# A two-layer diffusion backbone on one core: scaling ahead of the output split, squares in quarter buffers, and token transposes ahead of the logits

## The chip, the core and the metric

The kernel runs on one core of a Trainium2 chip. The metric is the device time of one launch in microseconds (us). Three runs of the kernel before took 1660.24, 1662.55 and 1663.87 us, median 1662.55.

## What is computed

Two layers of a transformer trunk over 256 latent tokens and 256 context tokens of width 1024, in float32. The even layer mixes tokens with a gated short convolution beside a four-head latent attention, then a dense SwiGLU. The odd layer mixes with six-head differential attention beside a Fourier transform, then a mixture of 8 SwiGLU experts, two for each token. Each sub-layer is wrapped in RMS norms with a shift, a scale and a gate. Cut to what the change touches:

```python
def _rms_norm(x, g):
    y = x * lax.rsqrt(jnp.mean(x * x, axis=-1, keepdims=True) + EPS)
    return y * g

def _mla_block(qb, k, v):
    s = jnp.einsum('bqhd,bkhd->bhqk', qb, k) * MLA_SCALE
    p = jax.nn.softmax(s, axis=-1)
    return jnp.einsum('bhqk,bkhd->bqhd', p, v)

# layer, for the latent stream (the context stream likewise in the even layer)
x = x + g1 * _rms_norm(y, norm_g[1])
h2 = _modulate(_rms_norm(x, norm_g[2]), sh2, sc2)
x = x + g2 * _rms_norm(ffn(h2), norm_g[3])
# experts
logits = h @ router_w
top_v, top_i = lax.top_k(logits, TOP_K)
```

## The kernel before

The activations lie with features on the 128 partitions, in 8 chunks, and tokens along the free dimension: 0 to 255 latent, 256 to 511 context. Each engine has its own program, written out by hand; they meet at semaphores only, so an engine does its work in exactly the order in which its block lists it. Weights come in pieces of 1 MB (128 x 2048) through SyncE's queue into 11 slots of the tensor `raw`. ScalarE copies a piece to a rounded half `wh` and VectorE subtracts to get `wl` (both `split`), and TensorE multiplies in three passes (`mm3`: high by high, high by low, low by high). In the dense and expert layers TensorE runs on end in this way. Between them lie stretches in which the engines hand small pieces of work to each other. The change touches four of them.

**Latent attention** (`attention("mla", ...)` on all three engines, each with a loop over i). There are 16 units of work, one head by one block of 128 queries; the units of latent queries have 512 keys (units 0 to 3 and 8 to 11), those of context queries 256. In turn i TensorE makes the scores (of a pair of units at once, in even turns, once ScalarE has done the exponentials of the pair before), a `mod_piece` as a filler (a piece of the matrix that turns the conditioning vector into shifts and scales; ScalarE takes its rows with `rows`), the transposes of the probabilities of unit i-2, and the product with V of unit i-3. VectorE takes the maximum of unit i and scales it (`negmax`), subtracts for the low half of the output of unit i-3 (`out_e`, al), and multiplies the probabilities of unit i-1 by their inverse sum (`scaled_e`). ScalarE makes the exponentials of unit i (`exp_e`), copies the transposed probabilities of unit i-2, and rounds the output of unit i-3 to `ah` (`out_e`). The waits that matter:

```python
                        act.wait_ge(s_("negmax"), i + 1)
                        if i >= 2:
                            act.wait_ge(s_("turned"), i - 1)
```

so the exponentials of unit i wait until TensorE has transposed unit i-2, whose buffer they write.

**Sums of squares.** For every norm ScalarE squares a chunk into one of two halves of `sq` (`square`) and TensorE sums it over the partitions with a matrix of ones (`sum_square`, one float32 matmul, which is two passes on the array). Two buffers, so `square` waits for the sum of two chunks before:

```python
                if j >= 2:
                    act.wait_ge(ssq_done, j - 1)
```

`root` turns the sum into the inverse root (Ln, then Exp), and VectorE goes on with `residual` (x is updated) or `modulate` (the normed, scaled input of the next matmuls: VectorE multiplies, ScalarE scales and rounds, VectorE subtracts, which releases TensorE chunk by chunk). The order of all squares is the list SQ_ORDER. N_E2C is the norm of the context stream ahead of the dense SwiGLU, N_EFL and N_EFC are the latent and context norms of its result, N_O1L and N_O1C those ahead of the odd layer.

**Between the layers.** The 8 banks of PSUM hold the result of the dense layer. VectorE copies them to `y2_e` in four copies of two banks: banks 4 and 5, 6 and 7, and, after ScalarE has squared banks 0 to 3 straight from PSUM, 0 and 1, 2 and 3. The sums are put together in bank 4, so the first sum waits for the first copy. ScalarE then squares N_EFL, two chunks of N_EFC, does the root of N_EFL, the other six of N_EFC, and N_O1L behind them.

**Routing.** After the odd layer's mixer VectorE makes the four quarters of the new tokens (`tok_new`); TensorE transposes each (`new_tokens`), VectorE or ScalarE copies it to x, and TensorE multiplies with the router (`logits`, 4 float32 matmuls of 8 columns a quarter). VectorE then ranks the experts, TensorE counts (L2364 to L2367), VectorE makes the selection matrix, and `first_gather` collects the first expert's tokens. `keep_busy(bank, times)` issues matmuls of 512 columns whose result nobody reads; each is two passes.

Of the kernel before, what the change touches and what calls it, by code (L numbers as in the profile page):

```python
# [27 lines left out]
P = 128  # L28
D = 1024
KD = D // P  # L30
TL = 256
# [130 lines left out]
def each(n, count=KD):  # L162
# [8 lines left out]
            + [(N_EYC, 2)] + each(N_E2L)[6:] + [(N_EYC, 3)] + each(N_E2C) + each(N_EFL) + each(N_EFC)  # L171
            + each(N_O1L) + each(N_O1C))
# [21 lines left out]
def bank_of(n):  # L194
    return NORM_BANK.get(n, 4)

# [73 lines left out]
def build(nc, x_d, vec_d, cst_d, rope_d, dft_d, uq_d, ukv_d, w_d, out_d):  # L270
# [3 lines left out]
    with ExitStack() as ctx:  # L274
# [70 lines left out]
        pr_e = area(12544, 2, T)  # L345
# [3 lines left out]
        mod_row_at = [area(2048, 2, 256), area(14592, 2, 256), area(8192, 2, 256)]  # L349
        mod_row = lambda q: mod_row_at[0 if JOINT * q < NORM_MODS else 1 if JOINT * q < GAP_MODS else 2][:, q % 2, :]  # L350
# [34 lines left out]
        hh = lambda g: sq[:, 1, (g % 2) * 256:(g % 2 + 1) * 256]  # L385

# [158 lines left out]
        def _(act):  # L545
# [133 lines left out]
            def attention(name, units, exp, out, begun=None):  # L679
# [26 lines left out]
            def exp_e(i):  # L706
                n = units[i][2]
                return act.activation(pr_e[:, i % 2, 0:n], ps[:, i % 2, 0:n], ACT.Exp, bias=small[:, 16 + i:17 + i],
# [7 lines left out]
            attention("mla", units, exp_e, out_e)  # L716
# [92 lines left out]
            def sub_square(k, half):  # L809
                n = N_EFC if half else N_EFL  # L810
                if half or k >= 4:
                    act.wait_ge(sem("y2_dve"), (3, 3, 4, 4, 1, 1, 2, 2)[k])
# [273 lines left out]
        def _(dve):  # L1086
# [244 lines left out]
            def attention(name, units, scale, scaled, out, begun=None):  # L1331
# [3 lines left out]
                for i in range(len(units) + 3):  # L1335
# [15 lines left out]
                    if i >= 3:  # L1351
                        out(i - 3)
                    if 1 <= i <= len(units):
# [4 lines left out]
                        scaled(u).then_inc(s_("probs"), 1)  # L1358

            units = mla_units()  # L1360

            def scaled_e(i):
                n = units[i][2]
                return dve.tensor_scalar(pr_e[:, i % 2, 0:n], pr_e[:, i % 2, 0:n], small[:, 32 + i:33 + i], None, ALU.mult)
# [1247 lines left out]
```

## Time and profile before

| | us |
|---|---|
| median of 3 runs (lowest, highest) | 1662.55 (1660.24, 1663.87) |
| the profiled execution, its own time | 1663.6 |
| its span, first to last instruction | 1661.9 |
| TensorE busy | 1615.5 (97%) |
| VectorE busy | 1127.4 (68%) |
| ScalarE busy | 928.7 (56%) |
| mean granted clock of TensorE | 0.994 |

A share of the span says little here: TensorE shows busy nearly always, since the ends of its matmuls are modelled and a pass that waits for its operand's predecessor counts. What matters is what TensorE waits for in the four stretches, and whether the work behind them starts as soon as they end. PE stands for TensorE, PEld for its weight loads, DVE for VectorE, ACT for ScalarE, SP for SyncE and POOL for GpSimd.

### The profile page before, as it was taken

The page shows a single profiled execution, that of the slowest core. Times are in us where ns is not written, and L with a number is a line of the kernel's source. Part 1 is how long each engine was busy: PE and PEld are TensorE (multiplying, and loading weights), DVE is VectorE, ACT ScalarE, POOL GpSimd, SP SyncE. Part 2 cuts the span into 40 slices and gives each one's busy share as a digit, 9 for nine tenths or more (in the row PEclk, how much of TensorE's full clock was granted, in tenths as well). Part 3 has the DMA queues.
Part 4 walks back from the last instruction along what each step waited for, and adds up shares of the span by engine and source line. Part 5 has one row for each costly group of instructions (what it writes and reads, how often), then busy time and mean ns, then how long its engine had stood idle before and what let it go on. Part 6 is the DMA issues. An engine that isn't in the chain of part 4 may idle for free.

```text
span 1661.9 us, 22634 instructions
## 1 busy us (share of the span) xinstructions
PE 1615.5 (97%) x8260; PEld 1298.2 (78%) x8260; DVE 1127.4 (68%) x1503; ACT 928.7 (56%) x1335; POOL 45.1 (3%) x66
## 2 busy tenths in 40 slices
PE   7999989999999999899998999999999999999997
PEld 3884469888888888688786888888888888888886
DVE  5442433549563333553667999899999999899998
ACT  4314323622122322552566778777778777787875
POOL 0000000210000000000101000000000000000000
PEclk9999999999999999999999999999999999999999
DMA  8523631696533222352136999999999999999982
GB/s 348 206 76 127 253 128 51 220 402 239 202 140 114 102 102 101 136 210 102 29 123 271 420 421 419 392 375 382 367 389 359 399 362 399 373 377 391 374 341 78
DMA packets 68379, 427.82 MB, mean 257 GB/s; under 512 B 8785, under 2 KB 12625, under 8 KB 20305
## 3 DMA queue, kind: packets, MB, share of 16 engines
q1 hardware_dynamic: 60000, 396.93, 61.6%
q0 software_dynamic: 8304, 29.90, 4.8%
q8 instruction: 47, 0.77, 0.2%
q14 instruction: 28, 0.22, 0.1%
HBM read 403.20 MB, written 23.61 MB: 257 GB/s over the span
## 4 chain that ended last, share of the span: by engine, by line
PE 92%; DVE 3%; ACT 2%; DMA 1%; issue 1%; SPq 0%; DVEq 0%; ACTq 0%
PE ps L1878 27%; PE ps L1880 27%; PE ps L1879 27%; PE ps L1896 1%; PE ps L2076 1%; PE ps L1942 1%; DMA raw<-in_w 1%; PE ps L2423 1%; PE ps L2120 1%; PE ps L2141 1%; PE ps L1907 1%; PE ps L2109 1%; PE ps L2261 1%; PE ps L2145 0%; PE ps L2385 0%
## 5 line engine op out<-in xcount | busy, mean ns | idle before, releaser
L1704 DVE TENSOR_TENSOR wl<-raw,wh 128x1024 fp32r<-128x1024 f32 x522 | 615.6, 1222 | 60.2 <-ACT wh L1004 52.8
L1004 ACT ACTIVATE wh<-raw 128x1024 fp32r<-128x1024 f32 x522 | 525.0, 1057 | 95.0 <-PE ps L1880 94.9
L1878 PE MATMUL ps<-wh,ah 128*128 128x512 f32 (+1 forms) x864 | 329.5, 381 | 0.5
L1880 PE MATMUL ps<-wh,al 128*128 128x512 f32 (+1 forms) x864 | 320.5, 371 | 0.0
L1879 PE MATMUL ps<-wl,ah 128*128 128x512 f32 (+1 forms) x864 | 319.8, 370 | 0.0
L1878 PE MATMUL ps<-ah,wh 128*128 128x512 f32 (+1 forms) x784 | 282.9, 361 | 4.7 <-DVE al L1133 3.9
L1880 PE MATMUL ps<-ah,wl 128*128 128x512 f32 (+1 forms) x784 | 274.8, 350 | 0.0
L1879 PE MATMUL ps<-al,wh 128*128 128x512 f32 (+1 forms) x784 | 274.4, 350 | 0.0
L1103 DVE TENSOR_TENSOR wl<-raw,wh 128x1024 fp32r<-128x1024 f32 x120 | 141.5, 1221 | 104.4 <-ACT wh L566 104.4
L1880 PEld LDWEIGHTS ps<-wh,al 128*128 128x128 f32 x864 | 162.7, 188 | 28.8
L1878 PEld LDWEIGHTS ps<-wh,ah 128*128 128x128 f32 x864 | 162.8, 188 | 28.5 <-issue 3.6
L1879 PEld LDWEIGHTS ps<-wl,ah 128*128 128x128 f32 x864 | 163.2, 189 | 26.1 <-issue 0.7
L1878 PEld LDWEIGHTS ps<-ah,wh 128*128 128x128 f32 x784 | 148.2, 189 | 31.0 <-issue 5.5
L1879 PEld LDWEIGHTS ps<-al,wh 128*128 128x128 f32 x784 | 148.2, 189 | 20.1 <-issue 0.7
L1880 PEld LDWEIGHTS ps<-ah,wl 128*128 128x128 f32 x784 | 148.1, 189 | 19.8
L566 ACT ACTIVATE wh<-raw 128x1024 fp32r<-128x1024 f32 x120 | 120.3, 1053 | 38.0 <-PE ps L1880 27.5
L1878 PE MATMUL ps<-wh,sh 128*128 128x512 f32 x352 | 137.9, 392 | 1.7 <-DVE sl L1717 1.7
L1880 PE MATMUL ps<-wh,sl 128*128 128x512 f32 x352 | 137.5, 391 | 0.0
L1879 PE MATMUL ps<-wl,sh 128*128 128x512 f32 x352 | 136.9, 389 | 0.0
L1878 PEld LDWEIGHTS ps<-wh,sh 128*128 128x128 f32 x352 | 66.1, 188 | 15.5 <-DVE sl L1717 2.1
L1880 PEld LDWEIGHTS ps<-wh,sl 128*128 128x128 f32 x352 | 66.1, 188 | 13.9
L1879 PEld LDWEIGHTS ps<-wl,sh 128*128 128x128 f32 x352 | 66.1, 188 | 13.5
(282 smaller groups left out, 1565.8 us busy)
## 6 DMA issues: line engine op xcount, KB each, us to landing
raw<-in_w SPq DMA_DIRECT2D x372, 1024.0 KB, 6.9
sent<-raw POOLq DMA_DIRECT2D x16, 512.0 KB, 24.0
back<-raw POOLq DMA_DIRECT2D x16, 512.0 KB, 25.0
x<-sent POOLq DMA_DIRECT2D x7, 512.0 KB, 11.6
back<-x POOLq DMA_DIRECT2D x7, 512.0 KB, 8.4
x<-in_x SPq DMA_DIRECT2D x2, 1024.0 KB, 8.1
raw<-in_ukv SPq DMA_DIRECT2D x1, 1024.0 KB, 7.4
ah<-flat_rows POOLq DMA_DIRECT2D x2, 512.0 KB, 7.0
```

The lines of the kernel that those rows point to most:

```text
L566: act.activation(wh[:, s % SPLITS, half(h)], slot(ring_slot("main", s))[:, half(h)], ACT.Copy).then_inc(w_hi, 1)
L1004: act.activation(wh[:, J % SPLITS, piece_half(h)], slot(J % SLOTS)[:, piece_half(h)], ACT.Copy).then_inc(w_hi, 1)
L1103: ins = dve.tensor_tensor(wl[:, s % SPLITS, half(h)], slot(ring_slot("main", s))[:, half(h)], wh[:, s % SPLITS, half(h)].bitcast(F32), ALU ...
L1704: ins = dve.tensor_tensor(wl[:, J % SPLITS, piece_half(h)], slot(J % SLOTS)[:, piece_half(h)], wh[:, J % SPLITS, piece_half(h)].bitcast(F3 ...
L1878: pe.matmul(out, lh, rh, start=start, stop=False)
L1879: pe.matmul(out, lh, rl, start=False, stop=False)
L1880: return pe.matmul(out, ll, rh, start=False, stop=stop)
L1896: mm = pe.matmul(ps[:, bank_of(n), 0:W], ones, sq[:, j % 2, i * W:(i + 1) * W], start=(k == 0 and i == 0), stop=(k == count - 1 and i == p ...
L1907: pe.matmul(ps[:, bank, :], ones, cst[:, 0:4, :].rearrange("p a b -> p (a b)"), start=True, stop=True)
L1942: mm = pe.matmul(ps[at:at + 32, 6 + q % 2, 0:256], cond_columns(k, j), w[:, k * 256:(k + 1) * 256], start=(j == 0 and k < 4), stop=(j == J ...
L2076: mm = pe.matmul(ps[:, n % 4, :], l, r, start=(k == 0), stop=(k == len(parts) - 1))
L2109: mm = pe.transpose(ps[:, tb + u % 2, b * P:(b + 1) * P], pr(u, b), ident)
```

## The change

It makes four edits.

1. Latent attention: a third buffer for the probabilities (`pr_e[i % 3]`; ScalarE waits for the transposes of unit i-3), and VectorE scales unit i-1 ahead of the subtraction for unit i-3. The third buffer takes the place of the rows of modulation at 14592, which go to `t2`.
2. Squares of 256 columns go to four quarters of `sq`; each waits for the sums of the squares that lay in its own columns. Squares of 512 columns keep the two halves.
3. Between the layers: the first copy from PSUM is cut in two (bank 4, then bank 5), the squares of the PSUM banks release the later copies one pair at a time, and the squares of N_O1L are put among the last four of N_EFC, on ScalarE and TensorE alike.
4. Routing: the four transposes ahead of the four logits, and `keep_busy(6, 2)` in place of `keep_busy(6, 4)`.

```diff
-            + [(N_EYC, 2)] + each(N_E2L)[6:] + [(N_EYC, 3)] + each(N_E2C) + each(N_EFL) + each(N_EFC)
-            + each(N_O1L) + each(N_O1C))
+            + [(N_EYC, 2)] + each(N_E2L)[6:] + [(N_EYC, 3)] + each(N_E2C) + each(N_EFL) + each(N_EFC)[:4]
+            + [e for k in range(4) for e in ((N_O1L, k), (N_EFC, k + 4))] + each(N_O1L)[4:] + each(N_O1C))
...
+WIDE = (N_E1, N_Q, N_KV, N_EYL, N_EYC)
+
+def sq_columns(j):
+    return range(T * (j % 2), T * (j % 2) + T) if SQ_ORDER[j][0] in WIDE else range(TL * (j % 4), TL * (j % 4) + TL)
+
+def sq_older(j):
+    return max([0] + [i + 1 for i in range(j) if set(sq_columns(i)) & set(sq_columns(j))])
...
-        pr_e = area(12544, 2, T)
+        pr_e = [area(at, T) for at in (12544, 13056, 14592)]
...
-                if j >= 2:
-                    act.wait_ge(ssq_done, j - 1)
-                W = int(np.prod(src.shape[1:]))
-                act.activation(sq[:, j % 2, 0:W], src, ACT.Square).then_inc(sq_ready, 1)
+                if sq_older(j):
+                    act.wait_ge(ssq_done, sq_older(j))
+                act.activation(squares_at(j), src, ACT.Square).then_inc(sq_ready, 1)
...
-                        if i >= 2:
-                            act.wait_ge(s_("turned"), i - 1)
+                        if i >= buffers:
+                            act.wait_ge(s_("turned"), i - buffers + 1)
...
-            for k in range(2, KD):
-                sub_square(k, 1)
+            sub_square(2, 1)
+            sub_square(3, 1)
             for k in range(KD):
                 next_square(N_O1L, k)
+                if k < 4:
+                    sub_square(k + 4, 1)
                 if k == 5:
                     root(N_EFC)
...
-                    if i >= 3:
-                        out(i - 3)
                     if 1 <= i <= len(units):
                         u = i - 1
                         dve.wait_ge(s_("exp"), u + 1)
                         cols = slice(sums + nm * u, sums + nm * (u + 1))
                         link(dve.reciprocal(small[:, cols], small[:, cols]))
                         scaled(u).then_inc(s_("probs"), 1)
+                    if i >= 3:
+                        out(i - 3)
...
-            for q in (2, 3, 0, 1):
-                if q < 2:
-                    dve.wait_ge(sq_ready, SQ_AT[N_EFL, 3] + 1)
-                dve.tensor_copy(y2_e[:, 2 * q:2 * q + 2, :], ps[:, 2 * q:2 * q + 2, :]).then_inc(sem("y2_dve"), 1)
-            dve.wait_ge(sem("y2_dve"), 4)
+            for a, b in ((4, 5), (5, 6), (6, 8), (0, 2), (2, 4)):
+                if a < 4:
+                    dve.wait_ge(sq_ready, SQ_AT[N_EFL, b - 1] + 1)
+                dve.tensor_copy(y2_e[:, a:b, :], ps[:, a:b, :]).then_inc(sem("y2_dve"), 1)
+            dve.wait_ge(sem("y2_dve"), 5)
...
-            sum_squares(N_EFC, range(2, KD))
-            sum_squares(N_O1L)
+            sum_squares(N_EFC, range(2, 4))
+            for k in range(KD):
+                sum_square(N_O1L, k)
+                if k < 4:
+                    sum_square(N_EFC, k + 4)
...
             for n in range(4):
                 new_tokens(n)
-                if n:
-                    logits(n - 1)
-            logits(3).then_inc(sem("logits_ps"), 1)
-            keep_busy(6, 4)
+            for n in range(4):
+                mm = logits(n)
+            mm.then_inc(sem("logits_ps"), 1)
+            keep_busy(6, 2)
```

Three places where the order on an engine changes. VectorE in latent attention, turns 4 and 5 of the loop, before (`small` are the maxima and sums, `raw` the probabilities, `al` the low half of the output; names in brackets are the semaphores waited for):

```order
L1347 TENSOR_REDUCE small<-ps 128x1 [waits mla_scores]
L1348 TENSOR_SCALAR small<-small 128x1 [waits dve_chain]
L1370 TENSOR_TENSOR al<-ps,ah 128x128 [waits mla_ohi]
L1357 RECIPROCAL small<-small 128x1 [waits mla_exp]
L1364 TENSOR_SCALAR raw<-raw,small 128x512 [waits dve_chain]
```

and now:

```order
L1363 TENSOR_REDUCE small<-ps 128x1 [waits mla_scores]
L1364 TENSOR_SCALAR small<-small 128x1 [waits dve_chain]
L1371 RECIPROCAL small<-small 128x1 [waits mla_exp]
L1380 TENSOR_SCALAR raw<-raw,small 128x512 [waits dve_chain]
L1386 TENSOR_TENSOR al<-ps,ah 128x128 [waits mla_ohi]
```

The subtraction moved behind the scaling of the same turn, and stands directly ahead of the next turn's maximum.

ScalarE between the layers, behind the root of N_EFL, as it is now (`sq<-raw` squares of N_EFC, `sq<-x` squares of N_O1L; before there were six of the first and then six of the second):

```order
L594 ACTIVATE sq<-x 128x256 [waits ssq_done,res_done]
L594 ACTIVATE sq<-raw 128x256 [waits ssq_done,y2_dve]
L594 ACTIVATE sq<-x 128x256 [waits ssq_done,res_done]
L594 ACTIVATE sq<-raw 128x256 [waits ssq_done,y2_dve]
L594 ACTIVATE sq<-x 128x256 [waits ssq_done,res_done]
L594 ACTIVATE sq<-raw 128x256 [waits ssq_done,y2_dve]
L594 ACTIVATE sq<-x 128x256 [waits ssq_done,res_done] x2
```

The last four squares of N_EFC moved in between the first ones of N_O1L.

TensorE in the routing, before (transposes of the new tokens are `cst,x`, logits `vec,x`):

```order
L2337 MATMUL ps<-cst,x 128x128 [waits tok_new]
L2337 MATMUL ps<-cst,x 128x128 x3
L2348 MATMUL ps<-vec,x 128x8 [waits x_act]
L2348 MATMUL ps<-vec,x 128x8 x3
L2337 MATMUL ps<-cst,x 128x128 [waits tok_new]
L2337 MATMUL ps<-cst,x 128x128 x3
L2348 MATMUL ps<-vec,x 128x8 [waits tok_copied]
```

and now:

```order
L2357 MATMUL ps<-cst,x 128x128 [waits tok_new]
L2357 MATMUL ps<-cst,x 128x128 x3
L2357 MATMUL ps<-cst,x 128x128 [waits tok_new]
L2357 MATMUL ps<-cst,x 128x128 x3
L2357 MATMUL ps<-cst,x 128x128 [waits tok_new]
L2357 MATMUL ps<-cst,x 128x128 x3
L2368 MATMUL ps<-vec,x 128x8 [waits x_act]
L2368 MATMUL ps<-vec,x 128x8 x3
L2368 MATMUL ps<-vec,x 128x8 [waits tok_copied]
```

Nothing is added or dropped there; two groups of logits moved behind two groups of transposes.

## Rows read from the trace of the kernel before

**Rows 1.** Page, part 4: shares of the chain that ended last.
```profile
PE 92%; DVE 3%; ACT 2%; DMA 1%; issue 1%; SPq 0%; DVEq 0%; ACTq 0%
```
**Rows 2.** Stretches: length, each engine's busy time (instructions), clock, DMA share, GB/s.
```profile
176.00:239.00 63.00, 53.16 (x418) 32.10 (x419) 24.64 (x86) 21.46 (x68) 0.00 (x0) 0.97 0.50 186
...
894.00:1661.00 767.00, 756.11 (x3426) 618.83 (x3424) 700.81 (x761) 596.60 (x737) 21.35 (x22) 1.00 0.93 364
```
**Rows 3.** Timeline, PE, latent attention: start, us, instruction, [idle before, releaser].
```profile
211.75 1.13 PE L2145 MATMUL ps<-raw 64*128 64x512 f32 x4
...
213.81 0.66 PE L2109 MATMUL ps<-cst,raw 128*128 128x128 f32 x4
...
216.97 0.66 PE L2109 MATMUL ps<-cst,raw 128*128 128x128 f32 x4 [2.06 <-DVE raw L1364]
...
218.57 2.08 PE L2141 MATMUL ps<-raw 128*128 128x256 f32 x4
...
227.07 1.12 PE L2141 MATMUL ps<-raw 128*128 128x256 f32 x4
```
**Rows 4.** Timeline, DVE, latent attention.
```profile
213.64 0.15 DVE L1348 TENSOR_SCALAR small<-small 128x1 f32<-128x1 f32 x1
216.03 0.29 DVE L1370 TENSOR_TENSOR al<-ps,ah 128x128 fp32r<-128x128 f32 x1 [2.25 <-ACT ah L713]
...
216.83 0.69 DVE L1347 TENSOR_REDUCE small<-ps 128x1 f32<-128x512 f32 x1
...
235.35 0.35 DVE L1364 TENSOR_SCALAR raw<-raw,small 128x256 f32<-128x256 f32 x1
```
**Rows 5.** Timeline, ACT, latent attention.
```profile
214.57 0.69 ACT L708 ACTIVATE raw<-ps,small 128x512 f32<-128x512 f32 x1 [4.34 <-PE ps L2109]
...
217.74 0.69 ACT L708 ACTIVATE raw<-ps,small 128x512 f32<-128x512 f32 x1 [1.47 <-DVE small L1348]
...
231.88 0.47 ACT L708 ACTIVATE raw<-ps,small 128x256 f32<-128x256 f32 x1 [1.38 <-DVE small L1348]
```
**Rows 6.** Timeline, ACT and DVE, ahead of the dense layer (squares of N_E2C).
```profile
302.78 0.42 ACT L580 ACTIVATE sq<-x 128x256 f32<-128x256 f32 x1 [1.15 <-PE ps L1896]
...
311.41 0.42 DVE L1133 TENSOR_TENSOR al<-raw,ah 128x256 fp32r<-128x256 f32 x1 [0.70 <-ACT ah L612]
```
**Rows 7.** Timeline, DVE, PE and ACT, between the layers.
```profile
676.85 2.36 DVE L1477 COPY raw<-ps 128x1024 f32<-128x1024 f32 x2 [6.90 <-PE ps L1880]
...
678.13 4.83 PE L1896 MATMUL ps<-sq,cst 128*128 128x256 f32 x16 [1.32 <-DVE raw L1477]
683.18 1.10 PE L1896 MATMUL ps<-sq,cst 128*128 128x256 f32 x4 [0.22 <-ACT sq L580]
...
683.38 0.46 ACT L598 ACTIVATE rinv<-ps,small 128x256 f32<-128x256 f32 x1
...
694.36 0.47 ACT L598 ACTIVATE rinv<-ps,small 128x256 f32<-128x256 f32 x1 [0.92 <-PE ps L1896]
```
**Rows 8.** Timeline, PE and DVE, routing.
```profile
873.49 1.88 PE L1907 MATMUL ps<-cst 128*128 128x512 f32 x4
...
880.24 3.14 PE L2348 MATMUL ps<-vec,x 128*128 128x8 f32 x16
883.23 5.73 PE L1907 MATMUL ps<-cst 128*128 128x512 f32 x8
888.79 0.29 PE L2364 MATMUL ps<-small,cst 128*128 128x16 f32 x2
...
890.09 3.84 PE L2377 MATMUL ps<-t,x 128*128 128x128 f32 x32 [0.34 <-DVE t L1619]
...
885.58 0.17 DVE L1615 TENSOR_SCALAR small<-small 128x16 f32<-128x16 f32 x1
```
**Rows 9.** Stretches in the routing and in attention, for the granted clock.
```profile
880.00:884.00 4.00, 4.00 (x21) 3.71 (x20) 1.29 (x5) 2.71 (x6) 0.00 (x0) 0.57 1.01 414
...
218.00:222.00 4.00, 3.99 (x21) 2.19 (x23) 1.01 (x4) 1.18 (x4) 0.00 (x0) 0.57 0.01 2
```

More of the change, by code:

```diff
@@ L348, in build @@
         first_sq = lambda k: sq[:, k, :] if k < 2 else area(2560 + T * (k - 2), T) if k < 5 else area(6160 + T * (k - 5), T)
-        mod_row_at = [area(2048, 2, 256), area(14592, 2, 256), area(8192, 2, 256)]
-        mod_row = lambda q: mod_row_at[0 if JOINT * q < NORM_MODS else 1 if JOINT * q < GAP_MODS else 2][:, q % 2, :]
+        mod_row_at = [area(2048, 2, 256), t2[:, :].rearrange("p (a b) -> p a b", a=2), area(14592, 2, 256), area(8192, 2, 256)]
+        mod_row = lambda q: mod_row_at[sum(JOINT * q >= n for n in (NORM_MODS, ATT_MODS, GAP_MODS))][:, q % 2, :]
         pick_rows = small[:, 64:64 + 2 * JOINT]
@@ L385, in build, with squares_at @@
         hh = lambda g: sq[:, 1, (g % 2) * 256:(g % 2 + 1) * 256]
+        def squares_at(j):
+            cols = sq_columns(j)
+            return sq[:, :, :].rearrange("p a t -> p (a t)")[:, cols[0]:cols[-1] + 1]
         def vc(name, a=0, b=None):
@@ L677, in _, with attention @@
                 act.activation(dst, ps[:, n % 4, :], ACT.Copy).then_inc(sem("proj_ready"), 1)
-            def attention(name, units, exp, out, begun=None):
+            def attention(name, units, exp, out, begun=None, buffers=2):
                 s_ = lambda k: sem(f"{name}_{k}")
@@ L707, in exp_e @@
                 n = units[i][2]
-                return act.activation(pr_e[:, i % 2, 0:n], ps[:, i % 2, 0:n], ACT.Exp, bias=small[:, 16 + i:17 + i],
+                return act.activation(pr_e[i % 3][:, 0:n], ps[:, i % 2, 0:n], ACT.Exp, bias=small[:, 16 + i:17 + i],
                                       scale=MLA_SCALE, accum_out=small[:, 32 + i:33 + i])
@@ L714, in out_e @@
                                ).then_inc(sem("mla_ohi"), 1)
-            attention("mla", units, exp_e, out_e)
+            attention("mla", units, exp_e, out_e, buffers=3)
             def out_unit(u):
@@ L1363, in scaled_e @@
                 n = units[i][2]
-                return dve.tensor_scalar(pr_e[:, i % 2, 0:n], pr_e[:, i % 2, 0:n], small[:, 32 + i:33 + i], None, ALU.mult)
+                return dve.tensor_scalar(pr_e[i % 3][:, 0:n], pr_e[i % 3][:, 0:n], small[:, 32 + i:33 + i], None, ALU.mult)
             def out_e(u):
@@ L1895, in sum_square @@
                 for i in range(parts):
-                    mm = pe.matmul(ps[:, bank_of(n), 0:W], ones, sq[:, j % 2, i * W:(i + 1) * W], start=(k == 0 and i == 0),
+                    mm = pe.matmul(ps[:, bank_of(n), 0:W], ones, squares_at(j)[:, i * W:(i + 1) * W], start=(k == 0 and i == 0),
                                    stop=(k == count - 1 and i == parts - 1))
@@ L2225, in _ @@
             sum_squares(N_EFL)
+            pe.wait_ge(sem("y2_dve"), 2)
             sum_squares(N_EFC, range(2))
-            pe.wait_ge(sem("y2_dve"), 2)
+            pe.wait_ge(sem("y2_dve"), 3)
             mod_piece(GAP_MODS)
-            sum_squares(N_EFC, range(2, KD))
-            sum_squares(N_O1L)
+            sum_squares(N_EFC, range(2, 4))
[3 more added lines that the diff above has]
+                    sum_square(N_EFC, k + 4)
             mod_piece(GAP_MODS + 1)
             mod_piece(GAP_MODS + 2)
-            pe.wait_ge(sem("y2_dve"), 4)
+            pe.wait_ge(sem("y2_dve"), 5)
             def turn(t):
```

4 lines of the change are left out of this document (2 added, 2 removed).

## The prediction

> **What bounds the kernel now.** I read the shares of the chain first. TensorE has 92% of the chain that ended last [rows 1], but that alone doesn't say whether it worked or waited inside its busy time, so I read the stretches next. The expert layer is two fifths of the time, with TensorE busy 756.11 of 767 us, and nothing in it is edited [rows 2]: whatever is won ahead of it moves it forward and no more. Latent attention is the opposite: 63 us in which TensorE is busy 53.16, VectorE 24.64 and ScalarE 21.46 [rows 2], so three engines hand small steps round a ring, and each wait in the ring is a wait of the program. The third thing to read is the timeline of the four stretches, for what ends each wait. The profiled execution took 1663.6 us, 1.05 above the median 1662.55; I sum against it and take 1.05 off.
>
> **Latent attention, edit 1.** Take the turns of units 10 and 11. The scores of both end at 212.88 [rows 3], and VectorE has the scaled maximum of unit 10 at 213.79 [rows 4]. ScalarE could begin its exponential there but begins at 214.57 [rows 5], since it waits for the transposes of unit 8, which end at 214.47 [rows 3]: 0.74 us for the missing buffer. ScalarE then copies and rounds, which releases VectorE's subtraction at 216.03 [rows 4]. Behind it VectorE scales unit 9, and only at 216.83 takes the maximum of unit 11 [rows 4], which releases the exponential at 217.74 [rows 5], and that the next scores at 218.57 [rows 3]. Meanwhile TensorE sat idle 2.06 us for the probabilities of unit 9 [rows 3]. Now unit 9 is scaled as soon as the maximum of unit 10 is out, so those probabilities wait for nothing, and the maximum of unit 11 follows the subtraction directly. The subtraction takes 0.29, so 0.5 of the 0.80 between 216.03 and 216.83 goes, with the 0.74 of the buffer some 1.25 us a pair. VectorE gains a wait too: its next maximum stands behind a subtraction that waits for ScalarE's rounding. That was so before, with the scaling in between, so it costs nothing new.
> The same walk for the other pairs gives less where units have 256 keys: 1.0, 0.3, 0.45, 1.25 and 0 for the pairs between units 4 and 15. The tail gives more: unit 15's exponential starts at 231.88 [rows 5] and lasts under 0.7, but its scaling comes at 235.35 [rows 4], 2.7 later, because every scaling stands behind a subtraction two units older. Transposes and products of the last units keep TensorE for part of it; I take 2.2. Sum: 5.2.
> There is a clock term. Behind the idle 2.06 us TensorE runs at a granted 0.57 of full speed between 218 and 222 [rows 9], that is at its 1.2 GHz level for most of it. Scores of 256 keys took 2.08 there against 1.12 at the full 2.4 GHz [rows 3]; with the second half of the scores that is 1.5 us. With the idle time gone this may not come back; I take half of it, 0.8. Attention: **-6.0**, bounds -3.5 (half of the tail and the pairs) and -7.
>
> **Squares of N_E2C, edit 2.** Ahead of the dense layer VectorE and ScalarE modulate the latent chunks, and ScalarE squares a context chunk between them. It stalls for a sum two squares back: 1.15 us at 302.78 [rows 6], and again at the later chunks, so VectorE's last low half comes at 311.41, after a wait [rows 6]. Without stalls VectorE is the limit: two products, a subtraction and an update, 1.40 us a chunk. The third chunk would be at 302.2 and the eighth at 309.2 to 309.7: **-1.7**. The bound above is 0: TensorE has sums of its own here. The bound below is -2.
>
> **Between the layers, edits 2 and 3.** Everything here waits for the 24 sums of N_EFL, N_EFC and N_O1L. Two chunks take TensorE 4 passes, which here run 683.18 to 684.22, 0.26 a pass [rows 7], so 24 chunks are 48 passes, 12.5 us, and the filler among them 1.0. The first sum starts at 678.13 and waits for a copy of two banks that starts at 676.85 and lasts half of 2.36 [rows 7]. A copy of one bank lasts half as long again plus overhead, 0.65 to 0.7: the start moves to 677.55. If then TensorE never waited, the last sum would be out at 691.05 plus the drain, against a last root at 694.36 [rows 7]. It will wait some: VectorE's four or five copies still have to end (unchanged 4.7 us in all) ahead of the first squares of N_EFC, the root of N_EFL moves from 683.38 [rows 7] only to about 682.0, and ScalarE does the root of N_EFC just ahead of the last two squares of N_O1L. Walking it through, I get the last root at 691.8: **-2.5**, bounds -1.2 (the root of N_EFL's shift alone) and -3.3. The later stages in the odd layer are the same work in the same order.
>
> **Routing, edit 4.** Before, TensorE works without a pause from the first transposes to the end of the logits at 883.38, so their order cannot bring the end forward: 16 transposes and 32 passes are the same sum. It moves logits behind the last new tokens, which adds 0.1 to 0.3. What does count is the filler behind them: `keep_busy` with 8 passes takes 5.73 us at 883.23, VectorE has the mask at 885.75, and TensorE counts at 888.79 [rows 8], 3.0 late. Four passes take 2.87 at this speed, or 1.88 as in the row at 873.49 [rows 8]. They end about when the mask is out, 2.4 after the logits. So the count comes 2.4 to 2.9 behind the logits rather than 5.4. Less the 0.2: **-2.3**, bounds -3 and +0.5 (below).
> Here a rule speaks against the edit. First the rows: the granted clock is 0.57 between 880 and 884 [rows 9], after the tiny logit matmuls, and full again ahead of the gather, which takes 3.84 us for 32 passes [rows 8]; in between lay the 8 passes. A logit pass took 3.14/16 = 0.20 us at the low level, a pass of the gather 3.84/32 = 0.12 at the full one; both load a full set of weights, so by these rows a slow gather costs 32 x 0.08 = 2.6, and at most a doubling of its 3.84. The Trainium skill, "TensorE: Matmul & The Clock Gate", section "Part 1: The HAM clock gate", says that the array's full clock is released by sustained activity and taken back when it is missing. By that rule half of the filler might leave the gather at half speed, and this term would be about +0.5 rather than -2.3.
>
> **Sum.** 6.0 + 1.7 + 2.5 + 2.3 = 12.5 us. 1663.6 - 12.5 = 1651.1 against the profiled execution; less 1.05 it is 1650.0.
>
> **Rivals.**
> - *The clock stays low* through the gather. For: the rows of the routing above. Against: four passes at half speed are still 2.87 us of unbroken work. Routing gives +0.5 instead of -2.3: 1662.5 - 9.7 = **1652.8**; with the low stretch in attention back too, 1653.6.
> - *Attention doesn't follow.* The wait of the third buffer is gone in the order, but subtractions of the outputs may back up behind ScalarE, and products wait for them (two banks). Then only the tail or less is won: 1662.5 - 6.5 - 1.5 = **1654.5**. Against: each step of the ring has slack over its busy time [rows 2].
> - *Handed back in the experts.* The expert layer streams 364 GB/s at a DMA share of 0.93 [rows 2]. If an earlier start only made TensorE wait for weights, the end would not move: **1662**. Against: TensorE is busy 756 of 767 there, so it isn't short of weights.
> - *Slower.* The mechanism is the clock once more. If, without the passes taken out, the low level held beyond the gather into the experts, each us of their matmuls would take two. The 10.2 us won elsewhere less 2.9 for the gather are used up once 7 us worth of expert matmuls have run so, and 13 us worth give 1662.5 + 5.7 = **1668**. Against: by the row at 227.07 [rows 3] and by the gather at 890.09 [rows 8] the full level was back 9 and 10 us after each low stretch began, with less than dense work in between.
>
> **How the numbers follow.** Forecast 0.70, clock low 0.12, attention short 0.09, handed back 0.05, slower 0.04. 0.2% is 3.3 us, about what a measurement of this kernel can tell from no change. The first three are faster by more: 0.91; handed back is within it: 0.05; slower: 0.04. The forecast's terms at their far bounds give -15.3, and with the runs' own spread 1646.5 is a fair low end; the high end takes in both smaller rivals and attention at its near bound with the second term at 0: 1656.5.
>
> **What would show it.** In the profile after: no idle time of TensorE for VectorE's scaling amid attention, and attention down from the 63 us of [rows 2] to about 57; ScalarE's squares of N_E2C without waits, and the last low half of the latent chunks 1.5 to 2 us earlier relative to its first; the last root between the layers 15 us after the end of the dense layer, not 17.5; the count 2.4 to 2.9 us after the logits, and the clock full in the gather. The prediction is wrong if one of these stretches shrinks and the next one grows by as much, or if the expert layer takes over 768 us.

## Result and profile after

The changed kernel took 1652.14 us in the median of 4 runs (1651.8 to 1653.16), the kernel before 1663.21 in 4 runs beside it (1660.24 to 1667.46). The ratio is 0.9933, interval 0.9916 to 0.9949: 11.1 us faster (8.5 to 14). The forecast was 1650.0, range 1646.5 to 1656.5. The profiled execution took 1652.2 us with a span of 1650.2, against 1663.6 and 1661.9: 11.7 off the span. Three executions among those below, at 1815, 2754 and 7762 us with a granted clock of 0.85, 0.60 and 0.20, are left out of every comparison.

Where they went, by the start times of TensorE's instructions in the two timelines (each row ends where the next begins; the dense layer ends with its last product). The row of N_E2C runs over the dense layer's first products, one group for each latent chunk; between them stand the sums of N_E2C:

| stretch | before | changed | difference | forecast |
|---|---|---|---|---|
| start to first scores | 176.85 | 179.07 | +2.22 | 0 |
| latent attention, to the output projection | 61.38 | 54.51 | -6.87 | -6.0 |
| output projection, to the first dense product | 61.64 | 62.33 | +0.69 | 0 |
| N_E2C, first dense product to past the eighth sum | 13.58 | 11.50 | -2.08 | -1.7 |
| rest of the dense layer | 363.36 | 363.35 | 0 | 0 |
| between the layers, to the first product of the odd layer | 20.62 | 16.86 | -3.76 | -2.5 |
| odd layer, to the first transpose of the new tokens | 178.82 | 178.67 | -0.15 | 0 |
| routing, to the first expert product | 17.43 | 15.52 | -1.91 | -2.3 |
| experts and end | 768.22 | 768.39 | +0.17 | 0 |

The four stretches of the forecast gave 14.6 us where it had 12.5. Two that it left at nothing took 2.9 back.

Stretches of the changed kernel, attention and experts (columns as in [rows 2]), and shares of its chain, page, part 4:

```profile
178.20:234.35 56.15, 51.05 (x418) 31.30 (x419) 24.64 (x87) 22.27 (x68) 0.00 (x0) 1.00 0.56 208
881.80:1650.20 768.40, 757.89 (x3429) 620.62 (x3427) 700.53 (x760) 596.69 (x737) 21.66 (x22) 1.00 0.93 363
```
```profile
PE 92%; DVE 4%; ACT 2%; DMA 1%; issue 1%; SPq 0%; DVEq 0%; ACTq 0%
```

The 63 us of [rows 2] are 56.15; the experts take what they took. The shares of the chain have hardly moved from [rows 1]: they don't show a gain of 0.7%; the stretches do.

Attention, timeline of PE, every instruction of the stretch that waited:

```profile
184.65 1.98 PE L2157 MATMUL ps<-raw 128*128 128x512 f32 x4 [0.70 <-ACT raw L722]
196.91 1.13 PE L2157 MATMUL ps<-raw 128*128 128x256 f32 x4 [0.48 <-ACT raw L722]
210.11 1.98 PE L2157 MATMUL ps<-raw 128*128 128x512 f32 x4 [1.38 <-ACT raw L722]
217.52 1.13 PE L2157 MATMUL ps<-raw 128*128 128x256 f32 x4 [0.93 <-ACT raw L722]
```

No transpose waits for VectorE's scaling any more, where one waited 2.06 us in [rows 3]. What is late next is the exponential (L722). VectorE in the turn that answers to [rows 4]:

```profile
214.17 0.49 DVE L1380 TENSOR_SCALAR raw<-raw,small 128x512 f32<-128x512 f32 x1
215.58 0.29 DVE L1386 TENSOR_TENSOR al<-ps,ah 128x128 fp32r<-128x128 f32 x1 [0.92 <-ACT ah L727]
215.79 0.68 DVE L1363 TENSOR_REDUCE small<-ps 128x1 f32<-128x512 f32 x1
216.50 0.15 DVE L1364 TENSOR_SCALAR small<-small 128x1 f32<-128x1 f32 x1
```

The maximum (L1363) follows the subtraction (L1386) after 0.21 us (215.58 to 215.79), not 0.80, and the subtraction waits for ScalarE's rounding as foreseen.

N_E2C: ScalarE squares four chunks without a wait (1.15 us in [rows 6]), timeline of ACT. Before it, in the output projection, TensorE has a wait that is new, timeline of PE:

```profile
299.09 0.42 ACT L594 ACTIVATE sq<-x 128x256 f32<-128x256 f32 x1
300.49 0.42 ACT L594 ACTIVATE sq<-x 128x256 f32<-128x256 f32 x1
302.02 0.40 ACT L594 ACTIVATE sq<-x 128x256 f32<-128x256 f32 x1
303.29 0.42 ACT L594 ACTIVATE sq<-x 128x256 f32<-128x256 f32 x1
```
```profile
284.55 1.03 PE L1912 MATMUL ps<-sq,cst 128*128 128x256 f32 x4
287.08 0.70 PE L1912 MATMUL ps<-sq,cst 128*128 128x256 f32 x2 [0.43 <-ACT sq L594]
```

Between the layers, timelines of PE and ACT (answers to [rows 7]). The sums start 0.75 us after the copies at 670.80 and then run on end; the last root comes 13.75 after 670.80, not 17.5:

```profile
671.55 4.58 PE L1912 MATMUL ps<-sq,cst 128*128 128x256 f32 x20 [0.79 <-DVE raw L1493]
676.06 1.07 PE L1958 MATMUL ps<-raw 128*32 128x256 f32 x16
677.06 5.90 PE L1912 MATMUL ps<-sq,cst 128*128 128x256 f32 x24
683.38 1.13 PE L1912 MATMUL ps<-sq,cst 128*128 128x256 f32 x4 [0.42 <-ACT sq L594]
```
```profile
684.55 0.47 ACT L612 ACTIVATE rinv<-ps,small 128x256 f32<-128x256 f32 x1 [0.92 <-PE ps L1912]
```

Routing, timeline of PE, and two stretches for the granted clock (answers to [rows 8, 9]):

```profile
866.29 2.55 PE L2357 MATMUL ps<-cst,x 128*128 128x128 f32 x16 [0.88 <-DVE x L1605]
868.68 3.64 PE L2368 MATMUL ps<-vec,x 128*128 128x8 f32 x32
872.17 2.73 PE L1923 MATMUL ps<-cst 128*128 128x512 f32 x4
874.75 0.61 PE L2384 MATMUL ps<-small,cst 128*128 128x16 f32 x2
...
876.56 5.49 PE L2397 MATMUL ps<-t,x 128*128 128x128 f32 x32
```
```profile
872.00:874.00 2.00, 2.00 (x7) 0.84 (x6) 1.51 (x8) 1.97 (x5) 0.00 (x0) 0.81 1.02 422
874.00:880.00 6.00, 6.00 (x26) 5.22 (x25) 3.76 (x10) 2.17 (x4) 0.00 (x0) 0.50 0.82 343
```

The count (L2384) starts 2.43 us behind the logits' end at 872.32, as forecast, not 5.4. But the clock is at its lower level, 1.2 GHz, from inside the filler (873.2) until shortly before the end of the gather (880.1): 5.49 us for its 32 passes against 3.84. That is the rival "the clock stays low". It costs 1.66 us in the gather and 0.51 in the small matmuls of the count. Half of that is made good by the logits, which escaped the low stretch: 7.13 us from the first transpose to their end before, 6.03 now. The filler gives -2.98 and the logits -1.10, the count takes 0.51 and the gather 1.66: together the -1.91 of the table.

### The profile page after: what moved, and what is told of

Same layout as the page of the kernel before. It is cut to its first block, busy times and chain, and to the rows that moved or that the text cites. A ratio compares the mean times of both kernels' runs of the same rounds, so it can differ in the third digit from the quotient of the medians.

```text
span 1650.2 us, 22626 instructions
## 1 busy us (share of the span) xinstructions
PE 1613.1 (98%) x8256; PEld 1300.7 (79%) x8256; DVE 1127.3 (68%) x1504; ACT 928.5 (56%) x1335; POOL 45.3 (3%) x66
## 4 chain that ended last, share of the span: by engine, by line
PE 92%; DVE 4%; ACT 2%; DMA 1%; issue 1%; SPq 0%; DVEq 0%; ACTq 0%
PE ps L1894 27%; PE ps L1896 27%; PE ps L1895 27%; PE ps L1912 2%; PE ps L2092 1%; PE ps L1958 1%; PE ps L2443 1%; DMA raw<-in_w 1%; PE ps L2157 1%; DVE small L1361 1%; PE ps L2136 1%; DVE raw L1551 0%; PE ps L2161 0%; PE ps L2405 0%; DVE raw L1550 0%
## 5 line engine op out<-in xcount | busy, mean ns | idle before, releaser
L1896 PEld LDWEIGHTS ps<-wh,sl 128*128 128x128 f32 x352 | 66.0, 188 | 13.9
```

The lines of the kernel that those rows point to most:

```text
L1896: return pe.matmul(out, ll, rh, start=False, stop=stop)
```

## Experiments

All twelve were timed beside the kernel before, in three groups. Its median was 1664.57 beside attention_only, third_buffer_only, order_only and squares_only, 1663.30 beside routing_only, longer_filler, logits_between and split_behind_squares, and 1664.33 beside the other four. "Same clock" is explained under the last of them.

**Edit 1 whole and in parts.** Each is the kernel before with: all of edit 1; or the buffer alone (`pr_e[i % 3]`, `i - buffers + 1`, the rows in `t2`); or the order alone:

```diff
-                    if i >= 3:
-                        out(i - 3)
                     if 1 <= i <= len(units):
...
                         scaled(u).then_inc(s_("probs"), 1)
+                    if i >= 3:
+                        out(i - 3)
```

> The kernel before with edit 1 alone (third buffer of probabilities and the scaling ahead of the subtraction). Attention is measured from the first scores to the first matmul of the output projection: 61.4 us before, 54.5 in the changed kernel. Ring theory: the waits of the ring are gone wherever the rest of the kernel stands, so 56.2 without a low-clock stretch less, 54.7 if the low stretch at 218 is gone as well; the stretches behind it keep their lengths, so the time falls by 5 to 7 us. Clock theory: part of the 6.9 us won in the changed kernel is the clock's alone and is paid back elsewhere (there a low stretch stood at 135 to 139 instead), so attention takes 54.5 to 56 but the time falls by 4 to 5 us only, with a low stretch of 3 to 4 us in another place.

> The kernel before with the third buffer of probabilities alone; the scaling stays behind the subtraction. By my walk of the ring the exponentials start earlier, but the scaling still stands behind a subtraction that waits for ScalarE's rounding: attention 60.5 against 61.4, so 0.9 us (0.5 to 1.5). Rival: the buffer is the main wait and the order follows from it: 3 us or more.

> The kernel before with VectorE's scaling ahead of the subtraction alone, two buffers. By my walk: attention 57.2 against 61.4 us, that is 4.2 won, or 5.7 where the low-clock stretch at 218 goes with it. Rival: without the third buffer ScalarE's exponential waits for the transposes and the order brings 2 or less.

| | ratio (interval) | median | attention in the profile |
|---|---|---|---|
| attention_only | 0.9972 (0.9958 to 0.9986) | 1659.13 | 54.50 |
| third_buffer_only | 1.0007 (0.9991 to 1.0022) | 1665.22 | 58.57 |
| order_only | 0.9963 (0.9948 to 0.9978) | 1657.41 | 55.95 |

Three later profiles have the old attention and no low clock in it: 59.90, 59.88 and 59.91 us. Against these the ring won 5.40 by both parts, 3.95 by the order and 1.33 by the buffer: nearly a sum, as the walk said (5.2, 4.2, 0.9). The walk holds pair by pair too. From the first scores of one pair to those of the next the ring won (copies_and_order, the old attention, against attention_only):

| | pair of units 4, 5 | 6, 7 | 8, 9 | 10, 11 | 12, 13 | tail |
|---|---|---|---|---|---|---|
| forecast | 1.0 | 0.3 | 0.45 | 1.25 | 0 | 2.2 |
| both parts | 0.97 | 0.42 | 0.57 | 1.32 | 0.02 | 2.11 |
| buffer alone | 0.11 | 0.35 | 0.01 | 0.73 | 0.02 | 0.13 |
| order alone | 0.86 | -0.02 | 0.47 | 0.60 | 0.02 | 2.02 |

The tail is the order's, and in the pair of the prediction's walk (10 and 11) the buffer alone gives 0.73 and the order alone 0.60, where it had 0.74 and 0.5. What waits, timeline of PE, third_buffer_only and then order_only:

```profile
216.00 0.66 PE L2109 MATMUL ps<-cst,raw 128*128 128x128 f32 x4 [1.33 <-DVE raw L1364]
...
233.17 0.44 PE L2109 MATMUL ps<-cst,raw 128*128 128x128 f32 x2 [1.15 <-DVE raw L1364]
```
```profile
211.12 1.98 PE L2141 MATMUL ps<-raw 128*128 128x512 f32 x4 [1.38 <-ACT raw L708]
217.16 1.16 PE L2120 MATMUL ps<-raw 128*128 128x128 f32 x8 [0.53 <-ACT raw L697]
```

With the buffer alone the transposes still wait for the scaling. With the order alone none does, and ScalarE is late in its place. The buffer's 1.33 us are too few to be seen in the time, whose interval is 1.5 us faster to 3.7 slower.

The clock theory is right in part. In attention_only and order_only a low stretch stands at 135 to 140 us, ahead of attention, and none in it. But such stretches also stand there with the old attention (routing_only at 132 to 136), so it isn't the low stretch of attention that moved. The time of attention_only fell by 4.7 us (2.3 to 7.0), which can't tell the ring theory's 5 to 7 from the clock theory's 4 to 5.

**Edits 2 and 3.** The kernel before with both; with the quarters alone; with the copies and the mixed order alone.

> The kernel before with edits 2 and 3 (quarters of the square buffer, first copy cut in two, mixed order of the squares). Ping-pong theory: with two halves a square and its sum could only alternate, 0.63 us a square between the layers (1.26 for two), and with quarters TensorE goes at its own 0.25 a pass: the last root 13.7 us after the end of the dense layer instead of 17.5, and the eighth chunk of N_E2C 11.5 after the first instead of 13.6; against it stands a new wait of the last wide square ahead of the dense layer for the sum directly before it, +0.7. Sum: -5.1 us, time down by 4.5 to 5.5. Rival: the -3.8 between the layers came out of the earlier stretches (other arrival of weights, other clock) and is -2.5 here as forecast: time down by 3 to 4.

> The kernel before with edit 2 alone: quarters of the square buffer, the old order of the squares and the old four copies. Ping-pong theory: nearly all of the 3.76 us won between the layers is the end of the alternation of ScalarE and TensorE, so the stretch from the end of the dense layer to the first matmul of the odd layer takes 17.2 to 17.6 us here (20.62 before, 16.86 with edits 2 and 3); the first sum still starts 1.28 us after the copy of two banks begins. Order theory: without the mixed order ScalarE's squares of N_O1L wait for VectorE's residuals behind the last sums, and the stretch is 18.3 or more. N_E2C is as in the changed kernel (11.5 us from the first to the eighth chunk), the output projection 62.3. Time down by 4.5 to 5.5.

> The kernel before with edit 3 alone: first copy cut in two and the mixed order of the squares, with the two halves of the square buffer kept. Ping-pong theory: two squares and their sums still take 1.26 us, so only the earlier start of the sums is won: 20.1 us between the layers against 20.62, time down by 0.5. Order theory: 18.5 or less, time down by 2 or more.

| | ratio (interval) | median | projection | N_E2C to past the dense layer | between the layers |
|---|---|---|---|---|---|
| before | | | 61.64 | 376.94 | 20.62 |
| squares_only | 0.9964 (0.9949 to 0.9980) | 1657.91 | 62.33 | 374.86 | 16.89 |
| quarters_alone | 0.9957 (0.9943 to 0.9971) | 1657.54 | 63.83 | 374.85 | 17.43 |
| copies_and_order | 0.9985 (0.9973 to 0.9998) | 1661.39 | 61.64 | 376.94 | 20.09 |

(The 63.83 has a low clock at 238 to 242, 1.5 us.) The quarters bring 3.19 of the 3.76 between the layers, the copy 0.53 alone, the mixed order next to nothing: both expectations of the ping-pong theory hold in the profile, and the forecast's -2.5 was too small in every profile with quarters. In the time copies_and_order fell by 2.5 us (0.3 to 4.5) where 0.5 was expected; the stretches don't show where the rest came from. ScalarE in copies_and_order and then in quarters_alone, timeline of ACT, between the layers:

```profile
678.91 0.85 ACT L580 ACTIVATE sq<-raw 128x256 f32<-128x256 f32 x2 [0.41 <-PE ps L1898]
680.17 0.85 ACT L580 ACTIVATE sq<-raw 128x256 f32<-128x256 f32 x2 [0.41 <-PE ps L1898]
681.43 0.85 ACT L580 ACTIVATE sq<-raw 128x256 f32<-128x256 f32 x2 [0.41 <-PE ps L1898]
```
```profile
678.95 2.58 ACT L594 ACTIVATE sq<-raw 128x256 f32<-128x256 f32 x6 [0.86 <-PE ps L1910]
```

Two halves: two squares each 1.26 us, then a wait for a sum, over and over, since a square and the sum before it can only just alternate. Four quarters: six squares on end. The times of squares_only and quarters_alone fell by 6.7 and 6.8 us, where the stretches account for 5.1 and 4.6. The first interval (3.3 to 8.5 us) holds its sum, the second (4.8 to 9.5) just misses it; what the rest is I can't say.

**The wait ahead of the dense layer.** The changed kernel with one edit:

```diff
             out_unit(6)
-            split(M_GU + 1)
             for k in range(6, KD):
                 stream_square(N_E2L, k)
+            split(M_GU + 1)
```

> The changed kernel with one more edit: ScalarE squares the last two chunks of N_E2L ahead of the copy of the weight piece M_GU + 1 instead of behind it. Theory: with quarters the wide square ahead of them waits for the sum directly before it (one sum more than with halves), so it starts 0.8 us ahead of TensorE's next sum instead of 2.3, and the 2 us of copy behind it make TensorE wait 0.43 us at 287.08; with the copy behind the squares that wait is gone, and from the output projection to the first chunk of N_E2C it takes 61.6 instead of 62.33 us: 0.5 to 0.7 faster in the profile, at the edge of what the median can tell. Rival: VectorE's half of that piece, now later, holds up the residuals of N_EYC behind it, and the stage stays at 62.3 or grows.

Ratio 0.9918 (0.9903 to 0.9933), median 1650.44. The projection takes 61.64, as before, and the sum that waited at 287.08 doesn't, timeline of PE:

```profile
284.67 1.03 PE L1912 MATMUL ps<-sq,cst 128*128 128x256 f32 x4
286.61 0.60 PE L1912 MATMUL ps<-sq,cst 128*128 128x256 f32 x2
```

The theory holds to 0.01 us. The wide square and what it waited for, timelines of ACT and PE, before and then the changed kernel:

```profile
286.20 0.60 PE L1896 MATMUL ps<-sq,cst 128*128 128x256 f32 x2
286.90 0.60 ACT L580 ACTIVATE sq<-ps 128x512 f32<-128x512 f32 x1 [1.44 <-PE ps L1896]
```
```profile
283.05 0.60 PE L1912 MATMUL ps<-sq,cst 128*128 128x256 f32 x2
283.74 0.60 ACT L594 ACTIVATE sq<-ps 128x512 f32<-128x512 f32 x1 [5.77 <-PE ps L1912]
284.71 2.01 ACT L581 ACTIVATE wh<-raw 128x1024 fp32r<-128x1024 f32 x2
```

With two halves the wide square of out_unit(6) waited for the sum of the square two before it; with narrow squares in quarters, the narrow one directly before lies in its own half, so it waits one sum more (before, the square began 0.10 us after the fifth of six narrow sums; in the changed kernel 0.09 after the sixth), and everything behind it on ScalarE, the 2 us weight copy first of all, moves on with it. The new wait itself is still there in split_behind_squares; only the copy no longer stands between it and the next squares.

**Edit 4.** In this order: the kernel before with edit 4 alone; the changed kernel with `keep_busy(6, 4)`; with the logits between the transposes again and `keep_busy(6, 2)`; split_behind_squares with `keep_busy(6, 0)`; the changed kernel itself.

> The kernel before with edit 4 alone (transposes ahead of the logits, 4 passes of filler in place of 8). Read from the profiles so far: where no low-clock stretch falls into the routing, the kernel before takes 14.24 us from the first transpose to the first expert matmul (3.37 of it from the end of the logits to the count), and with edit 4 that should be 13.3, since the count then waits for VectorE's mask, 2.43 behind the logits. Filler theory: 0.9 won without a low stretch, up to 2.6 where one falls on the filler, so the time falls by 1 to 2.5. Clock theory: the shorter filler lets the low clock reach the count and the gather (1.81 and 5.25 us against 1.30 and 3.59 at the full clock) in most executions: -0.9 to +0.5.

> The changed kernel with 8 passes of filler again. Filler theory: 0.9 to 2.6 us slower than the changed kernel, the count 3.4 us behind the logits at the full clock and 5 at the low one. Clock theory: the gather is back at 3.59 us in every execution, and the time is the same or up to 1 us shorter than with 4 passes.

> The changed kernel with the logits between the transposes again, 4 passes of filler. If the order of the logits is worth nothing, the transposes and logits take 6.0 us as in the changed kernel (6.03) and the time is within 0.5 us of it. The rival is that the order won the 1.1 us by which this part was shorter in the changed kernel (7.13 before): then 7.1 us here, and 1.1 slower. I expect the first: 7.13 had a low-clock stretch in its last third, and two of the last four profiles with the old order show 5.99.

> The changed kernel with the copy of M_GU + 1 behind the squares, as in split_behind_squares, and no filler at all behind the logits. TensorE then idles 2.4 us until the mask is there, in place of 1.9 us of passes and a short idle time. Filler theory: the count comes 2.43 us behind the logits as with 4 passes, and where a low-clock stretch falls there nothing of it is spent on filler: same time as split_behind_squares, within 1 us. Clock theory: the idle time brings the low clock into the gather every time (1.7 us) and into the first expert matmuls as well, 2 to 4 us slower.

> The changed kernel itself, in the same call, so that its runs and mean granted clock stand beside the others'. If the time is base plus what the low clock costs, its runs are slower where the mean granted clock is lower, with about 1.2 us for each 0.001 of the mean clock as in the 100 runs before, and the median is 1651 to 1653. The 0.7 us of the wide square's wait stands in it and not in the kernel with the copy behind the squares.

| | ratio (interval) | median | to logits' end, to count, to gather, to experts |
|---|---|---|---|
| routing_only | 0.9986 (0.9973 to 0.9999) | 1662.25 | 6.03, 2.76, 1.65, 4.98 |
| longer_filler | 0.9930 (0.9916 to 0.9945) | 1651.88 | 6.03, 5.07, 1.29, 3.59 |
| logits_between | 0.9926 (0.9911 to 0.9942) | 1650.91 | 5.99, 2.43, 1.40, 5.22 |
| no_filler | 0.9921 (0.9903 to 0.9939) | 1650.61 | 6.03, 2.43, 1.81, 5.53 |
| changed_again | 0.9928 (0.9909 to 0.9946) | 1651.68 | 6.03, 2.90, 1.65, 3.60 |

routing_only fell by 2.3 us (0.2 to 4.5), inside the filler theory's 1 to 2.5, though its count came 2.76 behind the logits and not 2.43, since its filler ran at the low level. The cleanest comparison is longer_filler with changed_again: in both a low stretch begins at about 870 and ends before the gather. Timeline of PE, first of longer_filler, then of changed_again:

```profile
870.04 5.38 PE L1923 MATMUL ps<-cst 128*128 128x512 f32 x8
875.26 0.29 PE L2384 MATMUL ps<-small,cst 128*128 128x16 f32 x2
```
```profile
869.57 3.26 PE L1923 MATMUL ps<-cst 128*128 128x512 f32 x4
872.62 0.45 PE L2384 MATMUL ps<-small,cst 128*128 128x16 f32 x2
```

15.98 us of routing against 14.18: four passes less are worth 1.8 where the clock falls alike, on the filler. Without a low stretch the expectation was 0.9, and no profile with 4 passes is without one. Over all profiles: with 8 passes 14.24 without a low stretch (three kernels), 15.95 with one of 3.4 us (four), 17.43 with one of 6.8 us (before). With 4 passes 14.18 and 14.24 where a stretch of 3.4 us ends before the gather, 15.04 where it meets it (logits_between), 15.42 and 15.52 with one of 6.8. The gather ran slow in four of the six profiles with 4 passes or none, and in none of the eight with 8. The means are 15.50 with 8 passes and 14.88 with 4. So both theories hold a part: the shorter filler wins 0.6 us in the mean of the profiles and 1.8 where the low stretch falls alike, and what it can no longer do is cover a low stretch until it is over. Whether it also makes one likelier (six of six against five of eight) so few profiles can't tell. The medians of longer_filler and changed_again differ by 0.2 us and don't settle it.

The order of the logits is worth nothing: 5.99 against 6.03. The 7.13 before was the same order under a low clock. No filler at all brings nothing over 4 passes (1650.61 against 1650.44). TensorE idles, and works at the low level for most of the gather (until 876.7), timeline of PE, no_filler:

```profile
870.78 0.61 PE L2384 MATMUL ps<-small,cst 128*128 128x16 f32 x2 [2.44 <-DVE small L1631]
...
872.59 5.78 PE L2397 MATMUL ps<-t,x 128*128 128x128 f32 x32
```

In this one profile the gather is slow, as the clock theory says, but the first expert products aren't, and of its 2 to 4 us none shows in the time.

**Same clock.** Every execution comes with its mean granted clock, 0.990 to 0.997. I laid one straight line through the 180 executions of the three groups, with a level for each kernel: 1.15 us slower (within 0.07) for each 0.001 less, and what is left scatters by 1.4 us, where the runs of the kernel before scatter by 2.6. At the same clock, against before, each with a standard error (the fit's own uncertainty) of 0.5 to 0.7 us: attention_only -5.5, order_only -5.8, third_buffer_only 0.0, squares_only -6.6, quarters_alone -6.6, copies_and_order -1.9, routing_only -2.6, longer_filler -11.4, logits_between -13.4, changed_again -13.8, split_behind_squares -13.9, no_filler -14.5. The parts, 5.5 + 6.6 + 2.6 = 14.7, add up to the whole within their errors, which speaks against a gain that is given back later. 4 passes are 2.4 us faster than 8 here, with an error of 0.8. But the fit doesn't give the stretches back one by one: order_only 5.8 against 3.95 in the profile, third_buffer_only 0.0 against 1.33, squares_only 6.6 against 5.1, copies_and_order 1.9 against 0.5, each about three standard errors or more apart, and that stays open. It is a fit, and the mean clock is itself an outcome of the kernel; I take it as weak support for the profiles and not as proof.

## Why the prediction was right, point by point

The four mechanisms are there, each in a run of its own. That 12.5 forecast and 11.7 measured in the profile lie so close is luck in part: the four stretches gave 2.1 more than forecast, and a low stretch at the start and a wait of the change's own making took 2.9 back.

- **Latent attention, -6.0.** The ring: 5.2 forecast, 5.40 measured, and nearly the same pair by pair (the wait for the buffer is 0.78 us by the rows, 213.79 to 214.57, not 0.74). The clock: with the low stretch between 218 and 222 attention took 61.38, without one 59.90, so the stretch costs 1.48 (I read 1.5 off two rows); squares_only with two such stretches took 63.01. Half of it was a guess that these runs can't confirm. I wrote that it followed the idle 2.06 us; but of the six profiles with the scaling behind the subtraction, with idle times like these, only two have low stretches in attention (one before, two in squares_only). Of the eight with the new order none has. Fewer may well fall there now, which these numbers don't settle. In the profile pair the whole 1.5 came out of attention, and another low stretch stood at 136 to 140.
- **Start, 0.** This part of the sum was missing. Nothing there is edited, yet the first scores stood at 174.78 to 179.44 in the fourteen profiles. As far as the rows show, all of the 2.22 goes with the clock. Timeline of PE, before and then the changed kernel:

```profile
134.72 2.94 PE L1896 MATMUL ps<-sq,cst 128*128 128x512 f32 x6 [1.93 <-ACT sq L580]
```
```profile
135.42 4.51 PE L1912 MATMUL ps<-sq,cst 128*128 128x512 f32 x6 [1.93 <-ACT sq L594]
```

The same passes took 1.6 more under a low clock. The other 0.7 had come up by 31 us: there the changed kernel's profile is at the low level from 16.5 to 23.3 us, amid the matmuls that lead to the first root, and the one before from 23.8 to 27.2, over a filler. A forecast against one profiled execution inherits its luck.

- **Squares of N_E2C, -1.7.** Measured 2.08, in every kernel with quarters, just outside the bounds (0 to -2). The limit I named, VectorE's 1.40 us a chunk, is met exactly (its low halves start at 295.44, 296.84 and so on to 303.85), but the eighth follows the seventh after 0.86. So the last low half comes 9.27 us after the first and not 12.01: 2.7 earlier, where I had written 1.5 to 2. TensorE passes on only 2.08 of it, since from there its own products and sums run on end.
- **What I left out: +0.69.** I checked which squares the quarters free and not which they tie down. The edit's own words say it: a square waits for the sums of those that lay in its own columns. For a wide square behind a narrow one that is a tighter wait than before.
- **Between the layers, -2.5, bounds -1.2 to -3.3.** Measured 3.76, outside the bounds. The mechanism, fewer waits between squares and sums, was right and its size off. A pass was taken at 0.26 from a row of four; in the row of twenty at 671.55 it is 4.51 / 20 = 0.23, in the next 0.24; over 48 passes that is 1.1 of the 1.26 missed. And I left TensorE three quarters of a microsecond for waiting and the drain, where the rows show a wait of 0.42 and 0.1 of drain. I also took the two-buffer alternation for a few waits; it set the pace of all 24 squares, as copies_and_order shows.
- **Routing, -2.3, bounds -3 to +0.5.** Measured 1.91 in the pair, 1.8 where a low stretch falls alike on the filler, 0.6 in the mean of all profiles. The filler term came as worked out (count 2.43 behind the logits). The rival came with it (gather 5.25 to the next start, not 3.59), and half of it was made good by logits outside the low stretch, which I hadn't counted: I had taken 0.2 off for them, and what they showed was 1.1 of clock. So the number was near and its parts weren't.
- **Rivals.** Clock through the gather: it came in the profile of the changed kernel and in three others with the short filler, but at 1.66 us rather than 2.6, and beside the full gain of the filler, so the stretch is -1.9 and not +0.5. In eleven of the fourteen profiles a low stretch began between 2.8 us before and 4.6 us after the end of the logits, and in three, all with 8 passes, none did. It lasted 6.8 us behind 8 passes (before) as behind 4 or none (three profiles), and 3.4 in the other seven: 8 passes didn't end it sooner, they held the gather back until it was over. The rule cited from the Trainium skill, "TensorE: Matmul & The Clock Gate", section "Part 1: The HAM clock gate", is that sustained activity releases the full clock and its absence takes it back. The traces agree in that the low stretches follow the small logits; they don't show that 8 unbroken passes bring the clock back sooner than 4. Attention doesn't follow: no. Handed back in the experts: no, 768.22 and 768.39. By the letter of the prediction's last sign, an expert layer of over 768 us, it would be wrong; but the kernel before is over 768 by the same borders, and the 767 of [rows 2] begins 0.3 us later and ends 0.9 us short, so the sign was set too tight. In four of the other profiles the stretch takes 769.4 to 769.6, all of it behind the last matmul; I can't say why. Low clock into the experts: no, it is full again from 880.1 on.

## What to carry to other kernels

Where two engines pass small steps round a ring, write down for each wait what stands ahead of it on its engine; moving one instruction past another that waits (order_only) brought three times what another buffer did (3.95 against 1.33 us). When a shared buffer is cut finer, list for every user whom it now waits for, since some wait for more. And compare stretch by stretch at the same granted clock: the rest of the dense layer agreed to 0.01 us in all fourteen profiles and attention to 0.03 wherever no low stretch fell into it, while the odd layer took 177.9 to 180.7 and a single execution's total moved by several.

## What the runs showed of the hardware

- TensorE's low clock falls in different places of the same code. A stretch between 132 and 140 us stands in eight of fourteen profiles, in and out of all edits; the low stretches before the last 10 us add to between 3.4 and 20.5 us a profile.
- In all fourteen profiles the granted clock is at its lower level at the very end, in some for the last 8 us, where the experts end.
- 0.001 of the mean granted clock went with 1.15 us of time, and with that line taken out the scatter between executions of one kernel falls from 2.6 to 1.4 us.
- The version with the copy behind the squares is the best of those tried by its median (1650.44, 12.9 us under the kernel before beside it; ratio 0.9918). Its margin over the changed kernel is shown in the profile, 0.69 us, and is within the scatter in the time.
